# First expert layer: 26 groups of equal members, or 25 groups of 96, 64 and 32 places mixed

## The reference

```python
def _moe_ffn(h, w_router, b_router, we_gate, we_up, we_down, ws_gate, ws_up, ws_down):
    hf = h.reshape(-1, D)                                   # 256 x 1024
    s = jax.nn.sigmoid((hf @ w_router).astype(jnp.float32))
    _, idx = lax.top_k(s + b_router.astype(jnp.float32), TOP_K)      # 8 of 64
    s_sel = jnp.take_along_axis(s, idx, axis=-1)
    wts = s_sel / jnp.sum(s_sel, axis=-1, keepdims=True) * ROUTE_SCALE
    ...
        y = (jax.nn.silu(xb @ we_gate[e]) * (xb @ we_up[e])) @ we_down[e]
        return acc.at[rows].add(y * rw[:, None].astype(y.dtype)), None
    ...
    shared = (jax.nn.silu(hf @ ws_gate) * (hf @ ws_up)) @ ws_down
    return (acc[:nt] + shared).reshape(B, T, D)
```

## Time and profile before

| | us |
|---|---|
| three runs, median (lowest to highest) | 1557.53 (1555.62 to 1557.55) |
| profiled execution, span | 1555.2 |
| profiled execution, around its span | not listed; the median of the runs is 2.3 above the span |
| first expert layer's groups, from the first L1361 to the last L1228 | 324.46 to 810.00 |
| TensorE busy in 324.5 to 810.2 | 458.50 |
| VectorE and ScalarE busy there | 60.65 and 67.25 |

### The profile page before, as it was taken

The page is one execution under the profiler, slowest core; times in us unless marked ns, Lnnn a source line. Parts: engine busy times, 40 slices in busy tenths (PEclk is TensorE's granted clock), DMA queues, the critical chain, the costliest instruction groups (busy, mean ns, idle before and its releaser), DMA issues.

```text
span 1555.2 us, 19875 instructions
## 1 busy us (share of the span) xinstructions
PE 1255.3 (81%) x8092; PEld 644.6 (41%) x8092; DVE 360.8 (23%) x877; ACT 178.9 (12%) x340; POOL 95.2 (6%) x125
## 2 busy tenths in 40 slices
PE   4999889799989989989977988887565765765754
PEld 2763435456556556555536544433221221221211
DVE  1588452611111111111113243324000000000002
ACT  1210200311111111111110012012000000000001
POOL 2595000000000000000001000000000000000000
PEclk9999979999999999999997999998886887887787
DMA  9765992278999999999976412363999999999993
GB/s 364 274 273 212 397 413 106 97 265 320 380 420 420 420 420 421 420 421 418 421 306 221 170 47 108 145 272 123 423 421 421 421 422 421 422 422 422 422 422 141
DMA packets 83877, 507.48 MB, mean 326 GB/s; under 512 B 8262, under 2 KB 9510, under 8 KB 34260
## 3 DMA queue, kind: packets, MB, share of 16 engines
q1 hardware_dynamic: 82708, 502.98, 79.3%
q0 software_dynamic: 944, 3.29, 0.7%
q10 hardware_dynamic: 144, 0.07, 0.0%
HBM read 505.25 MB, written 1.06 MB: 326 GB/s over the span
## 4 chain that ended last, share of the span: by engine, by line
PE 56%; DMA 33%; DVE 6%; SPq 2%; issue 1%; ACT 1%; DVEq 0%; ACTq 0%
DMA W<-in_w_expert_down 12%; DMA W<-in_w_expert_up 10%; PE PS L1361 10%; DMA W<-in_we_up 8%; PE PS L936 5%; PE PS L1228 5%; PE PS L1374 4%; PE PS L1430 4%; PE PS L1215 3%; PE PS L1508 3%; PE PS L1520 3%; DMA W<-in_w_ada 3%; PE PS L890 2%; PE PS L1101 2%; PE PS L1390 2%; PE PS L1488 2%
## 5 line engine op out<-in xcount | busy, mean ns | idle before, releaser
L1508 PE MATMUL PS<-W,scr 128*32 128x512 f32 x1024 | 175.6, 850 | 130.6 <-DMA W<-in_w_expert_up 66.8
L1361 PE MATMUL PS<-W,scr 128*32 128x256 f32 (+2 forms) x2048 | 195.6, 399 | 24.5 <-DMA W<-in_we_up 22.7
L1990 DVE TENSOR_TENSOR scr<-scr,PS 128x256 f32<-128x256 f32 (+1 forms) x34 | 24.1, 708 | 670.5 <-PE PS L1508 387.1
L1361 PEld LDWEIGHTS PS<-W,scr 128*32 128x32 f32 (+2 forms) x2048 | 126.5, 132 | 101.7 <-issue 53.4
L1508 PEld LDWEIGHTS PS<-W,scr 128*32 128x32 f32 x1024 | 40.3, 148 | 265.1 <-issue 112.8
L1228 PE MATMUL PS<-scr 128*128 128x512 f32 x272 | 125.3, 603 | 2.6 <-ACT scr L785 2.6
L1520 PE MATMUL PS<-W,scr 128*32 128x512 f32 x512 | 71.2, 706 | 34.2 <-DMA W<-in_w_expert_down 33.2
L1215 PE MATMUL PS<-scr 128*128 128x128 bf16 x1632 | 96.7, 219 | 0.4 <-DVE scr L1974 0.4
L1374 PE MATMUL PS<-W,scr 128*32 128x512 f32 (+2 forms) x512 | 94.9, 597 | 0.7 <-DVE scr L1993 0.7
L1215 PEld LDWEIGHTS PS<-scr 128*128 128x128 bf16 x1632 | 93.9, 98 | 2.1 <-DVE scr L1945 1.2
L774 ACT COPY scr<-PS 128x512 f32<-128x512 f32 x68 | 39.9, 587 | 436.7 <-PE PS L1215 436.7
(11 more groups left out here) (411 smaller groups left out, 1111.3 us busy)
## 6 DMA issues: line engine op xcount, KB each, us to landing
W<-in_we_gate SPq DMA_DIRECT2D x64, 1024.0 KB, 19.1
W<-in_we_up SPq DMA_DIRECT2D x64, 1024.0 KB, 17.0
W<-in_we_down SPq DMA_DIRECT2D x64, 1024.0 KB, 16.0
W<-in_w_expert_gate SPq DMA_DIRECT2D x64, 1024.0 KB, 18.7
W<-in_w_expert_up SPq DMA_DIRECT2D x64, 1024.0 KB, 19.3
W<-in_w_expert_down SPq DMA_DIRECT2D x64, 1024.0 KB, 19.4
W<-in_w_ada SPq DMA_DIRECT2D x12, 4096.0 KB, 18.1
W<-in_w_in SPq DMA_DIRECT2D x6, 4096.0 KB, 14.4
```

The costliest lines, as they stand in the source:

```text
L1361: m = mm(PS[4 + kind][j * cap:(j + 1) * cap, 0:F1], hTe[:, k, j * cap:(j + 1) * cap], piece_view((g, kind, j))[:, k, :], start=(k == 0), s ...
L1508: m = mm(PS[bank][j * CAP2:(j + 1) * CAP2, :], hTe[:, k, j * CAP2:(j + 1) * CAP2], gu2[piece][:, j, kk, :], start=(k == 0), stop=(k == KD ...
```

## The change

The unit is now 32 places, four to a group, and a group lists its members as (position, units). The four fullest of the sorted experts get 96 places in place of 128, and one of the 32-place experts stands beside each. Most other groups hold one member of 64 places and two of 32. The table has 25 groups: the two static pairs, 14 groups of 64+32+32, 4 of 96+32, and 5 of 64+64, the last of which ends the list. A member of 96 places is multiplied as a tile of 64 columns and one of 32 (`column_tiles`).

```diff
+UNIT = 32
 STATIC1 = 4
-GROUPS1 = [(0, 2), (2, 2)]
-_one, _two, _four = 4, 8, 32
...
+WIDE1, HALF1 = 8, 32
+def first_layer_groups():
+    groups = [[(0, 2), (1, 2)], [(2, 2), (3, 2)]]
+    wide, half, single = STATIC1, WIDE1, HALF1
+    for t in range(14):
+        groups.append([(half, 2), (single, 1), (single + 1, 1)])
+        half, single = half + 1, single + 2
+        if t % 3 == 1 and wide < WIDE1:
+            groups.append([(wide, 3), (single, 1)])
+            wide, single = wide + 1, single + 1
+        elif t % 3 == 2 or t == 13:
+            groups.append([(half, 2), (half + 1, 2)])
+            half += 2
+    return groups
...
+def column_tiles(group):
+    for j, (_, at, cap) in enumerate(places(group)):
+        for size in (2 * UNIT, UNIT):
+            if cap >= size:
+                yield j, at, size
+                at, cap = at + size, cap - size
...
             def gate_and_up1(g):
...
                     for k in range(KD):
-                        for j in range(n):
-                            m = mm(PS[4 + kind][j * cap:(j + 1) * cap, 0:F1], hTe[:, k, j * cap:(j + 1) * cap],
+                        for j, at, size in column_tiles(GROUPS1[g]):
+                            m = mm(PS[4 + kind][at:at + size, 0:F1], hTe[:, k, at:at + size],
                                    piece_view((g, kind, j))[:, k, :], start=(k == 0), stop=(k == KD - 1))
...
             def down1(g):
...
                     for h in range(2):
-                        for j in range(n):
-                            m = mm(PS[6 + h][j * cap:(j + 1) * cap, :], aT[:, c, j * cap:(j + 1) * cap],
+                        for j, at, size in column_tiles(GROUPS1[g]):
+                            m = mm(PS[6 + h][at:at + size, :], aT[:, c, at:at + size],
                                    piece_view((g, 2, j))[:, c, h * 512:(h + 1) * 512], start=(c == 0), stop=(c == F1 // P - 1))
...
-                    for bound, rows in ((8.5, 64.0), (4.5, -64.0)):
+                    for bound, rows in ((WIDE1 + 0.5, float(UNIT)), (STATIC1 + 0.5, -float(UNIT))):
...
                 def slots(n, par):
-                    first, G = GROUPS1[n] if L == 1 else (n * G2, G2)
-                    cap = P // G
+                    if L == 1:
+                        parts = []
+                        for first, at, cap in places(GROUPS1[n]):
+                            if parts and parts[-1][3] == cap and parts[-1][0] + parts[-1][1] == first:
+                                parts[-1][1] += 1
+                            else:
+                                parts.append([first, 1, at, cap])
...
                     for b in range(NB):
...
+                        for first, G, at, cap in parts:
+                            ins = v.tensor_tensor(Sb[:, b, at:at + G * cap].rearrange("p (e s) -> p e s", e=G), outer(iota[:, 0:cap], G),
+                                                  inner(rank[:, b, bass.ds(first, G)], cap), ALU.is_equal)
+                        ins.then_inc(S["x_S"], 1)
```

More of the change, by code:

```diff
@@ L36, with places @@
 NG2 = E2 // G2
+UNIT = 32
 STATIC1 = 4
-GROUPS1 = [(0, 2), (2, 2)]
-_one, _two, _four = 4, 8, 32
[L43 to L54, removed]
-NG1 = len(GROUPS1)
+WIDE1, HALF1 = 8, 32
[11 more added lines that the diff above has]
+            half += 2
+    assert (wide, half, single) == (WIDE1, HALF1, E1), (wide, half, single)
+    return groups
+GROUPS1 = first_layer_groups()
+NG1 = len(GROUPS1)
+def places(group):
+    start = 0
+    for position, units in group:
+        yield position, start * UNIT, units * UNIT
+        start += units
+def column_tiles(group):
[4 more added lines that the diff above has]
+                at, cap = at + size, cap - size
 SLOTS, SLOT_WORDS, RING0 = 12, 2048, 0
-PIECES1 = [(-1, kind, 0) for kind in range(3)] + [(g, kind, j) for g, (_, n) in enumerate(GROUPS1) for kind in range(3) for j in range(n)]
+PIECES1 = [(-1, kind, 0) for kind in range(3)] + [(g, kind, j) for g, group in enumerate(GROUPS1) for kind in range(3) for j in range(len(group))]
 RING = {piece: ((RING0 + i) % SLOTS, i // SLOTS) for i, piece in enumerate(PIECES1)}
@@ L495, in load_piece @@
                 else:
[L496 removed]
+                    at = GROUPS1[g][j][0]
                     expert = at if at < STATIC1 else sp.value_load(order[0:1, at:at + 1], min_val=1, max_val=E1) - 1
@@ L1352, in gate_and_up1 @@
             def gate_and_up1(g):
-                n = GROUPS1[g][1]
-                cap = P // n
                 for kind in range(2):
-                    for j in range(n):
+                    for j in range(len(GROUPS1[g])):
                         landed((g, kind, j))
                     for k in range(KD):
-                        for j in range(n):
-                            m = mm(PS[4 + kind][j * cap:(j + 1) * cap, 0:F1], hTe[:, k, j * cap:(j + 1) * cap],
+                        for j, at, size in column_tiles(GROUPS1[g]):
+                            m = mm(PS[4 + kind][at:at + size, 0:F1], hTe[:, k, at:at + size],
                                    piece_view((g, kind, j))[:, k, :], start=(k == 0), stop=(k == KD - 1))
@@ L1899, in over_rows @@
                 else:
-                    step(v.tensor_scalar(over_from, over_idx, 32.5, 32.0, ALU.is_lt, ALU.mult))
-                    step(v.tensor_scalar(over_from, over_from, 32.0, None, ALU.add))
-                    for bound, rows in ((8.5, 64.0), (4.5, -64.0)):
+                    step(v.tensor_scalar(over_from, over_idx, HALF1 + 0.5, float(UNIT), ALU.is_lt, ALU.mult))
+                    step(v.tensor_scalar(over_from, over_from, float(UNIT), None, ALU.add))
+                    for bound, rows in ((WIDE1 + 0.5, float(UNIT)), (STATIC1 + 0.5, -float(UNIT))):
                         step(v.tensor_scalar(cap_tmp, over_idx, bound, rows, ALU.is_lt, ALU.mult))
@@ L1969, in slots @@
                 def slots(n, par):
-                    first, G = GROUPS1[n] if L == 1 else (n * G2, G2)
-                    cap = P // G
+                    if L == 1:
[5 more added lines that the diff above has]
+                                parts.append([first, 1, at, cap])
+                    else:
+                        parts = [[n * G2, G2, 0, CAP2]]
                     for b in range(NB):
-                        v.tensor_tensor(Sb[:, b, :].rearrange("p (e s) -> p e s", e=G), outer(iota[:, 0:cap], G),
-                                        inner(rank[:, b, bass.ds(first, G)], cap), ALU.is_equal).then_inc(S["x_S"], 1)
+                        for first, G, at, cap in parts:
+                            ins = v.tensor_tensor(Sb[:, b, at:at + G * cap].rearrange("p (e s) -> p e s", e=G), outer(iota[:, 0:cap], G),
+                                                  inner(rank[:, b, bass.ds(first, G)], cap), ALU.is_equal)
+                        ins.then_inc(S["x_S"], 1)
                     dve.wait_ge(S["x_S"], 2 * (n + before) + 2)
                     for b in range(NB):
-                        v.tensor_tensor(Sw[:, par, b, :].rearrange("p (e s) -> p e s", e=G),
-                                        Sb[:, b, :].rearrange("p (e s) -> p e s", e=G),
-                                        inner(wts[:, b, bass.ds(first, G)], cap), ALU.mult).then_inc(S["x_Sw"], 1)
+                        for first, G, at, cap in parts:
+                            ins = v.tensor_tensor(Sw[:, par, b, at:at + G * cap].rearrange("p (e s) -> p e s", e=G),
+                                                  Sb[:, b, at:at + G * cap].rearrange("p (e s) -> p e s", e=G),
+                                                  inner(wts[:, b, bass.ds(first, G)], cap), ALU.mult)
+                        ins.then_inc(S["x_Sw"], 1)
                 def body(g, par, last=False):
```

## The result

| | before | after |
|---|---|---|
| runs, median (lowest to highest), us | 1556.6 (1555.62 to 1557.55) | 1783.3 (1782.37 to 1783.88) |
| ratio, 95% interval | | 1.145 (1.1437 to 1.1464) |
| profiled span | 1555.2 | 1782.1 |
| the layer's groups, first product to last combine | 324.46 to 810.00 | 326.34 to 1037.72 |

The forecast was 1786, in 1736 to 1840.

What follows compares the result with a forecast made beforehand. Transfers bound the expert layer, TensorE close behind. Groups of 14.7, 17.3, 69.2 (four pairs), 592.2 (18 mixed) and 20.3 us (last pair) make 713.7 against 485.5, +228: span 1783, forecast 1786 us, range 1736 to 1840.

Steps and rivals of the forecast that it cites:

- VectorE, SP, the limits: Expert layer: four more small tensor_tensor per mixed group hidden, same 192 pieces issued by SP; 0 us added.
- The cost of a change: TensorE, expert products: each switch of tile width costs 0.14 us (to 64 columns) or 0.13 us (to 32).
- the exclusion: TensorE, mixed steps: the 64-wide tile runs alone, then the two 32-wide together; 2 x 0.43 us a step.
- the 64-wide term: Cost of switching to 64 columns: 0.10 us as measured plus 0.05 for loading weights, taken as 0.14 us.
- gate and up, mixed: 16 steps of 256 columns in a mixed group: 18.1 us in place of 7.0, +11.1.
- down, mixed: Four down steps of 512 columns in a mixed group: 8.0 us in place of 3.5, +4.5.
- mixed group: A group with 64- and 32-wide tiles, 18 of 25 groups: 32.9 us on TensorE in place of 17.3.
- what follows it: The rest of the kernel, 745 us, moves as a block behind the expert layer.
- The DMA rate: Through the expert layer, about 22.5/32.9 of 421 GB/s, some 270 to 290.
- Rival 1: Expert products: the two widths run side by side, transfers bound the layer, about -8 us, 1549 us; chance 0.15.
- Rival 2: Mixed groups: the granted clock falls to 1.2 GHz, +470 us more, 2256 us; chance 0.03.
- Rival 3: An expert with more than 96 tokens goes through the extra pass, some 35 us; chance 0.01.

Runs made afterwards that it cites:

- the runs with 3, 15 and 31 changes: Changed kernel with matmuls sorted by width within each product, 1700.38 us; with width changing after every two steps, 1735.26 us; the changed kernel itself, 1783.3 us.

## Why the prediction was right

**What bounds the kernel before.** Transfers, with TensorE close behind. The run with the new table and tiles of 32 shows it: a group less on TensorE, but only about 6 us less of time, where 17.3 left TensorE (its idle in 500 to 600 grew from 7.3 to 9.75 us).

**VectorE, SP, the limits: 0.** VectorE's busy time went from 60.65 to 63.86 us over the layer, and TensorE waited for it only 0.8 us in the first and 0.7 us in the last group, where it did so before too. Right.

**The cost of a change and the exclusion.** Forecast 0.14 and 0.13 us a change, and two widths one after the other. Measured 0.134 to 0.135 as the mean of both directions, and inside a step about 0.14 and 0.13 (the load rows above); and full exclusion. The parts of the 64-wide term, 0.10 and 0.05, add up to 0.15 and not to the 0.14 that was used; 0.15 would have put the forecast some 4 us higher. That two widths exclude each other was inference, since no step of before had two widths; the runs with 3, 15 and 31 changes settle it.

**The terms of the sum**, forecast and measured in us:

| | forecast | measured |
|---|---|---|
| gate and up, mixed | 18.1 | 18.06 |
| down, mixed | 8.0 | 7.94 |
| mixed group | 32.9 | 32.74 to 32.80 |
| first and second group | 14.7, 17.3 | 14.65, 17.24 |
| last pair | 20.3 | 20.3 (1017.43 to 1037.72) |
| the layer | 713.7 | 711.4 (326.34 to 1037.72) |
| what follows it | 745 | 744.4 |
| span | 1783 | 1782.1 |

The layer starts 1.9 us later than in the profile of before. That is not part of the change: the first group started between 323.94 and 328.04 in the profiles of the other kernels. So the span came out as close as it did partly by offset: the layer was 2.3 us shorter than forecast and the rest 0.8, and the late start put 1.9 back.

**The DMA rate** was forecast at 270 to 290 GB/s and is 269 over the layer. 22.5/32.9 holds for groups of three members alone; those of 96+32 load two experts in the same time, and pairs take 15 us of transfers in 17.3. All 192 pieces in 711.4 us would be 283 GB/s, but eleven of them had landed before the layer began. The forecast took 22.5/32.9 alone.

**The rivals.** Rival 1, 1549 us: it fell for this kernel, and its time came out where its condition was made true (1551 and 1552 with tiles of 32). Rival 2, the clock: granted clock 1.00 over the layer. Rival 3: no extra pass shows; there are 64 loads each of gate, up and down pieces, as before.

## What to carry to other kernels

Column tiles of one width cost nothing in these runs, be it one, two or four of them; two widths in one loop cost twice the streaming time and 0.135 us at each change. So cut every tile to the smallest width that occurs (a member of 64 as two of 32) and mix freely: that turned +227 us into -6 us. Look for it in the trace as a longer gap between two lines whose only difference is the tile. And where transfers are the bound, try to end the list with a group whose transfers last longer than its computation: here the runs with such an end were 4 to 6 us faster, though why isn't shown.

## What the runs showed of the hardware

A step of four float32 tiles of 32 columns, of two of 64 and of one of 128 all take 0.43 us at a granted clock of 1.00, and 16 of them 7.00 to 7.04 us. The Trainium skill, "TensorE: Matmul & The Clock Gate", Part 3, has a weight load overlapping a running matmul only when its row group differs. The runs here differ from that: with tiles of 32 columns and all 128 rows, four loads of 0.11 us on average (112.2 us for 3200) are done within 0.13 us (358.80 in the load rows above), while TensorE is busy for 10.00 of 10.00 us (370 to 380). So weights are loaded beside each other and under running matmuls, as long as the width is one. A change between 64 and 32 columns costs 0.13 to 0.14 us and no step runs both widths at once.
